# Hybrid parts that begin with products of the unnormed x

## The reference, cut to what matters

```python
h = rms_norm_2(x, mix_norm[l])              # x * rsqrt(mean(x*x) + eps) * w
z = h @ w_in                                # 1024 x 3592
hq, hf, hi, hg, fq, fk, fv, ff = split(z)   # 4 x 512 | 3 x 512 | 8
logf_h = logaddexp(log(lb), log1p(-lb) + log_sigmoid(hf)); k_h = (1 - lb) * sigmoid(-hf)
q_h = silu(hq); o_h = hgrn2_chunk_scan(q_h, k_h, hi, logf_h)
o_h = rms_norm_2(o_h, out_norm_w) * silu(hg)
logf_f = log_sigmoid(ff + fox_bf)           # forget gates of 8 heads
o_f = forgetting_attention(fq, fk, fv, logf_f)
x = x + concat(o_h, o_f) @ w_out
```

## Time and profile before

| | us |
|---|---|
| median of 3 runs (2647.03 to 2649.49) | 2648.58 |
| the profiled execution | 2646.76 |
| span of its trace | 2645.0 |
| PE busy / weight loads busy | 2586.8 / 2520.4 |
| DVE busy / ACT busy / POOL busy | 1669.6 / 1357.4 / 147.3 |
| mean granted TensorE clock, share of full | 0.996 |

### The profile page before, as it was taken

The page is one execution under the profiler, slowest core; times in us unless marked ns, Lnnn a source line. Parts: engine busy times, 40 slices in busy tenths (PEclk is TensorE's granted clock), DMA queues, the critical chain, the costliest instruction groups (busy, mean ns, idle before and its releaser), DMA issues.

```text
span 2645.0 us, 48803 instructions
## 1 busy us (share of the span) xinstructions
PE 2586.8 (98%) x21554; PEld 2520.4 (95%) x21554; DVE 1669.6 (63%) x1988; ACT 1357.4 (51%) x1687; POOL 147.3 (6%) x227
## 2 busy tenths in 40 slices
PE   8999999999999999999999999999999999999998
PEld 8989999899998999999999999989999999999998
DVE  5667556575576755676646656766656657764764
ACT  5745545554456544664545445555445436554543
POOL 4400000000000000430000000000000000000000
PEclk9999999999999999999999999999999999999999
DMA  7515565456544564543666665444766755344763
GB/s 217 168 33 161 193 236 162 145 175 226 182 160 144 183 226 158 162 132 112 197 241 177 192 224 179 129 159 133 199 195 185 198 192 160 112 143 130 195 195 128
DMA packets 429971, 451.97 MB, mean 171 GB/s; under 512 B 13346, under 2 KB 395024, under 8 KB 427584
## 3 DMA queue, kind: packets, MB, share of 16 engines
q1 hardware_dynamic: 417952, 416.12, 50.4%
q0 software_dynamic: 7312, 32.35, 3.5%
q10 hardware_dynamic: 4496, 0.39, 0.1%
HBM read 441.21 MB, written 7.60 MB: 170 GB/s over the span
## 4 chain that ended last, share of the span: by engine, by line
PE 86%; DVE 6%; ACT 5%; issue 1%; DMA 1%; POOL 1%; ACTq 0%; SPq 0%; DVEq 0%; POOLq 0%
PE ps L610 85%; ACT wH L1514 2%; DVE wL L2164 2%; ACT hidden_parts L1574 1%; DMA ring<-in_gdn_w_in 0%; POOL arena L512 0%; DVE arena L2737 0%; ACT L1541 0%; PE ps L1041 0%; DVE hT L2420 0%; PE ps L1259 0%; DMA arena<-tiles_out 0%; DVE sq L2247 0%; DVE arena L2428 0%; ACT sq L1783 0%
## 5 line engine op out<-in xcount | busy, mean ns | idle before, releaser
L2164 DVE TENSOR_TENSOR wL<-ring,wH 128x2048 fp32r<-128x2048 f32 x392 | 898.2, 2292 | 740.9 <-ACT wH L1514 740.5
L1514 ACT ACTIVATE wH<-ring 128x2048 fp32r<-128x2048 f32 x392 | 753.3, 1922 | 990.7 <-PE ps L610 988.7
L610 PE MATMUL ps<-hidden_parts,wH 128*128 128x256 f32 x6656 | 990.3, 277 | 4.4 <-ACT hidden_parts L1574 3.0
L610 PEld LDWEIGHTS ps<-hidden_parts,wH 128*128 128x128 f32 x6656 | 900.3, 188 | 6.4 <-issue 3.8
L610 PE MATMUL ps<-hidden_parts,wL 128*128 128x256 f32 x3328 | 693.3, 276 | 1.4 <-DVE wL L2164 1.3
L610 PEld LDWEIGHTS ps<-hidden_parts,wL 128*128 128x128 f32 x3328 | 521.9, 188 | 1.8 <-DVE wL L2164 1.8
L610 PE MATMUL ps<-hH,wH 128*128 128x256 f32 x2624 | 366.8, 281 | 6.8 <-DVE hH L2181 3.4
L610 PE MATMUL ps<-hH,wL 128*128 128x256 f32 x2624 | 358.3, 278 | 1.5 <-DVE wL L2164 1.5
L610 PE MATMUL ps<-hL,wH 128*128 128x256 f32 x2624 | 346.1, 278 | 0.0
L610 PEld LDWEIGHTS ps<-hH,wH 128*128 128x128 f32 x2624 | 328.5, 189 | 15.5 <-issue 13.2
L610 PEld LDWEIGHTS ps<-hH,wL 128*128 128x128 f32 x2624 | 326.1, 188 | 2.1 <-DVE wL L2164 2.0
(11 more groups left out here) (323 smaller groups left out, 1969.3 us busy)
## 6 DMA issues: line engine op xcount, KB each, us to landing
ring<-in_mlp_w SPq DMA_DIRECT2D x128, 1024.0 KB, 5.3
ring<-in_ffn_w_gate SPq DMA_DIRECT2D x88, 512.0 KB, 4.0
ring<-in_ffn_w_up SPq DMA_DIRECT2D x88, 512.0 KB, 5.3
ring<-in_ffn_w_down SPq DMA_DIRECT2D x44, 1024.0 KB, 5.1
ring<-in_gdn_w_in SPq DMA_DIRECT2D x32, 1024.0 KB, 5.9
ring<-in_w_in SPq DMA_DIRECT2D x28, 1024.0 KB, 5.4
hidden_parts<-mem_parts POOLq DMA_DIRECT2D x14, 1024.0 KB, 6.8
ring<-in_mlstm_w_in SPq DMA_DIRECT2D x12, 1024.0 KB, 5.3
```

What stands on the lines that cost most here:

```text
L610: return pe.matmul(o, l, r, start=start, stop=stop, **k)
L1514: f(wH[:, n % PARTS, :], ring[:, n % RING, :], ACT.Copy).then_inc(sem("high_split"), 1)
L2164: tt(wL[:, n % PARTS, :], ring[:, n % RING, :], wH[:, n % PARTS, :].bitcast(F32), ALU.subtract)\
```

## The change

- ACT (`late_start`) copies x times the norm's weights into `start_x[0]` (fp32r) instead of squaring first, empties the filler, makes the high part of slab 1, then squares xT, loads the table for ln and exp, and makes rs.
- DVE makes `start_x[1]`, the low part of slab 1, and the sum of squares over the chunks (`late_low`), then splits the 64 x 128 forget gate weights in two (`fox_w`).
- PE runs the whole filler first, then slab 0 alone, then slab 1; the two matmuls that end the sum of squares stand behind slab 1's products with the low part of x. The forget gates are 24 fp32r matmuls.
- Slabs 0 to 3 use `start_x`. DVE multiplies their sums by rs on the way from PSUM into qk (`scaled_out`), which ACT did without rs; ACT applies Silu to slabs 2 and 3 in SBUF.
- hT is still made (DVE, `normed`), and hH and hL from it (`normed_high` on ACT, `normed_low` on DVE) for slab 4 and later. PE waits for all of it ahead of slab 4.
- `start_x` lies where v_tok and gate are, so GpSimd's clearing of these waits for PE's end of slab 3.

```diff
+        start_x = (hidH[:, 24:32, :], hidH[:, 16:24, :])
+        fox_w = [flat_parts[:, at:at + DC * 8].rearrange("p (c n) -> p c n", c=DC) for at in (15424, 15488)]
 # GpSimd, hybrid
                     W.chain(pool.memset(qk[64:128, 12:16, :], 0.0))
+                    pool.wait_ge(sem("products_done"), group("w_in_2", i, HYBRID_ORDER[3]))
                     W.chain(pool.memset(gate[0:64, 4:8, :], 0.0))
 # TensorE, first_products
                 for k in range(DC):
                     both_halves(1, high_w[1], xL, k)
+                if behind_high:
+                    behind_high()
                 pe.wait_ge(sem("low_split"), n[1] + 1)
 # TensorE, hybrid
-                norm_sum(behind=6, filler=filled_before[("hybrid", l)], at=(0, 0, 0, 0, 10))
-                first_products("w_in_2", l, HYBRID_ORDER[0:2], DC, columns)
+                fill(filled_before[("hybrid", l)], 0, 2 * MEM_PIECES)
+                first_products("w_in_2", l, HYBRID_ORDER[0:2], DC, columns, src=start_x,
+                               together=False, behind_high=summed_norm)
...
-                        for k in range(DC):
-                            last = mm(ps[0:8, 0, 0:T], gw[:, 3 + l, k, 0:8], hT[:, k, :], k == 0, k == DC - 1)
+                        pe.wait_ge(sem("gate_split"), W.next("gate_split"))
+                        last = three(ps[0:8, 0, 0:T], [lambda k: fox_w[0][:, k, :], lambda k: fox_w[1][:, k, :]],
+                                     [lambda k: start_x[0][:, k, :], lambda k: start_x[1][:, k, :]], DC)
                     if n >= 4:
-                        pe.wait_ge(sem("evac"), W.next("evac"))
-                    (to_tokens if s in (4, 5) else to_channels)("w_in_2", l, s, bank_of(n))
+                        pe.wait_ge(sem("scaled_out"), W.next("scaled_out"))
+                    if n == 4:
+                        pe.wait_ge(sem("normH_ready"), W.next("normH_ready", 4))
+                        pe.wait_ge(sem("normL_ready"), W.next("normL_ready", 4))
+                    (to_tokens if s in (4, 5) else to_channels)("w_in_2", l, s, bank_of(n),
+                                                                src=start_x if n < 4 else (hH, hL))
 # ScalarE
+            def late_start(name, layer, j, gain, k0, filler):
+                for c in range(4):
+                    act.wait_ge(sem("x_ready"), W.next("x_ready"))
+                    for k in (2 * c, 2 * c + 1):
+                        ins = f(start_x[0][:, k, :], xT[:, k, :], ACT.Copy, scale=column(gain, k0 + k))
+                    ins.then_inc(sem("hH_ready"), 1)
+                empty_filler(filler)
+                split(slab_no[(name, layer, j)] + PARTS)
+                for c in range(4):
+                    f(sq[:, 2 * c:2 * c + 2, :], xT[:, 2 * c:2 * c + 2, :], ACT.Square).then_inc(sem("xsq_ready"), 1)
+                ln_exp()
+                act.wait_ge(sem("ss_ready"), W.next("ss_ready"))
+                rsqrt(ps[:, 2, 0:T], rs[:, :], D, "rs_ready")
 # ScalarE, hybrid
-                x_norm("w_in_2", l, HYBRID_ORDER[0], filler=filled_before[("hybrid", l)])
-                channels("w_in_2", l, 1, 4, chunks(qk, 4))
+                late_start("w_in_2", l, HYBRID_ORDER[0], "mix_norm_2", l * DC, filled_before[("hybrid", l)])
+                for n in range(2):
+                    ready("w_in_2", l, HYBRID_ORDER[n])
+                act.wait_ge(sem("scaled_out"), W.next("scaled_out", 2))
                 W.chain(f(glog, qk[:, 4:8, :], ACT.Abs))
                 W.chain(f(glog, glog, ACT.Exp, scale=-1.0))
                 f(glog, glog, ACT.Ln, bias=1.0).then_inc(sem("glog_ready"), 1)
+                normed_high()
 # VectorE, hybrid
-                x_norm("mix_norm_2", l * DC, "w_in_2", l, HYBRID_ORDER[0])
+                late_low("mix_norm_2", l * DC, start_x, "w_in_2", l, HYBRID_ORDER[0])
+                dve.wait_ge(sem("gates_in"), GATE_LOADS)
+                W.chain(dve.tensor_copy(fox_w[0], gw[:, 3 + l, :, 0:8]))
+                tt(fox_w[1], gw[:, 3 + l, :, 0:8], fox_w[0].bitcast(F32), ALU.subtract).then_inc(sem("gate_split"), 1)
...
                 dve.memset(pair[:, 0:4, :], 0.0)
...
+                refill("w_in_2", l, HYBRID_ORDER[0])
+                dve.wait_ge(sem("rs_ready"), W.next("rs_ready"))
+                scaled_out(0)
+                scaled_out(1)
+                normed("mix_norm_2", l * DC)
                 refill("w_in_2", l, 3)
                 dve.wait_ge(sem("gates_done"), W.next("gates_done"))
-                ts(r(1), ps[0:8, 0, 0:T], gbias[:, 2 + l:3 + l], None, ALU.add).then_inc(sem("fz_ready"), 1)
+                W.chain(tt(r(1), ps[0:8, 0, 0:T], rs[0:8, :], ALU.mult))
+                ts(r(1), r(1), gbias[:, 2 + l:3 + l], None, ALU.add).then_inc(sem("fz_ready"), 1)
+                normed_low()
                 dve.wait_ge(sem("glog_ready"), W.next("glog_ready"))
...
                 negative_cum(r(5)).then_inc(sem("rows_ready"), 1)
+                scaled_out(2)
                 refill("w_in_2", l, 0)
+                scaled_out(3)
```

More of the change, by code:

```diff
@@ L640, in bank_of, with first_products @@
                 return 4 + j % 4
-            def first_products(name, layer, js, c, at, src=(hH, hL), together=True):
+            def first_products(name, layer, js, c, at, src=(hH, hL), together=True, behind_high=None):
                 n = [slab_no[(name, layer, j)] for j in js]
@@ L1345, in hybrid @@
                     if n == 2:
-                        pe.wait_ge(sem("gates_in"), GATE_LOADS)
-                        for k in range(DC):
-                            last = mm(ps[0:8, 0, 0:T], gw[:, 3 + l, k, 0:8], hT[:, k, :], k == 0, k == DC - 1)
+                        pe.wait_ge(sem("gate_split"), W.next("gate_split"))
+                        last = three(ps[0:8, 0, 0:T], [lambda k: fox_w[0][:, k, :], lambda k: fox_w[1][:, k, :]],
+                                     [lambda k: start_x[0][:, k, :], lambda k: start_x[1][:, k, :]], DC)
                         last.then_inc(sem("gates_done"), 1)
                     if n >= 4:
-                        pe.wait_ge(sem("evac"), W.next("evac"))
-                    (to_tokens if s in (4, 5) else to_channels)("w_in_2", l, s, bank_of(n))
+                        pe.wait_ge(sem("scaled_out"), W.next("scaled_out"))
[4 more added lines that the diff above has]
+                                                                src=start_x if n < 4 else (hH, hL))
                 to_channels("w_in_2", l, 8, 1)
@@ L1564, in x_norm, with normed_high @@
                 empty_filler(filler)
+            def late_start(name, layer, j, gain, k0, filler):
[11 more added lines that the diff above has]
+                rsqrt(ps[:, 2, 0:T], rs[:, :], D, "rs_ready")
+            def normed_high():
+                for c in range(4):
+                    act.wait_ge(sem("h_ready"), W.next("h_ready", 2))
+                    f(hH[:, 2 * c:2 * c + 2, :], hT[:, 2 * c:2 * c + 2, :], ACT.Copy).then_inc(sem("normH_ready"), 1)
             def late_norm(name, layer, gain, k0, x_parts, between, filler=None):
@@ L1998, in hybrid @@
             def hybrid(l):
-                x_norm("w_in_2", l, HYBRID_ORDER[0], filler=filled_before[("hybrid", l)])
-                channels("w_in_2", l, 1, 4, chunks(qk, 4))
-                act.wait_ge(sem("evac"), W.next("evac", 2))
+                late_start("w_in_2", l, HYBRID_ORDER[0], "mix_norm_2", l * DC, filled_before[("hybrid", l)])
+                for n in range(2):
+                    ready("w_in_2", l, HYBRID_ORDER[n])
+                act.wait_ge(sem("scaled_out"), W.next("scaled_out", 2))
                 W.chain(f(glog, qk[:, 4:8, :], ACT.Abs))
@@ L2018, in hybrid @@
                 f(qk[:, 4:8, :], qk[:, 4:8, :], ACT.Sigmoid, scale=-1.0).then_inc(sem("hk_ready"), 1)
-                channels("w_in_2", l, 0, 6, chunks(qk, 0), func=ACT.Silu)
+                for s in range(2):
+                    ready("w_in_2", l, s)
+                    act.wait_ge(sem("scaled_out"), W.next("scaled_out"))
+                    v = qk[:, 2 * s:2 * s + 2, :]
+                    f(v, v, ACT.Silu)
                 channels("w_in_2", l, 3, 4, chunks(gate, 0), func=ACT.Silu)
@@ L2058, in hybrid @@
                         attention_slab(SLAB_ENDS[n - 1])
-                W.next("evac", 12)
                 square_pair(0, two(ps[:, 0, :]), "o_ready")
@@ L2197, in x_norm, with late_low @@
                     split(slab_no[(name, layer, j)] + PARTS)
-            def late_low(gain, k0, x_parts, name, layer):
+            def late_low(gain, k0, x_parts, name, layer, j=0):
                 for c in range(4):
@@ L2205, in late_low, with normed, normed_low @@
                     ins.then_inc(sem("hL_ready"), 1)
-                split(slab_no[(name, layer, 0)] + PARTS)
+                split(slab_no[(name, layer, j)] + PARTS)
                 sum_squares("xsq_ready", "xsq_summed")
+            def normed(gain, k0):
+                for c in range(DC):
```

(20 more changed lines are left out.)

## The result

| | before | changed |
|---|---|---|
| median of 15 runs | 2646.04 us | 2652.08 us |
| the profiled execution, its span | 2646.76, 2645.0 | 2651.15, 2649.4 |
| DVE busy / ACT busy | 1669.6 / 1357.4 | 1688.1 / 1361.9 |
| mean granted clock of TensorE | 0.996 | 0.993 |

The ratio is 1.0025, 95% interval 1.0019 to 1.0032: slower by some 6.6 us (5.0 to 8.5). Every ratio in this document is to runs of the kernel before that were taken beside it.

A forecast was written before the change was run, and what follows sets the result against it. PE was taken as the bound behind slab 5, with DVE exactly as late in front of it. Second part +2.5, first +0.3 and clock +1.0 made +3.8 us on 2648.58: 2652.4, range 2645.5 to 2657.

The forecast's parts named there:

- The start, the sum of squares, the gates: Layer 1: first product 1.06 us behind ACT, sum of squares ready 10.6 behind, gates 2.7 us on PE.
- the walk: Step-by-step timing of the first hybrid part: products start at the filler's end, 1613.6; PE asks for slab 4's low part at 1641.2.
- the list of signs: Expected trace evidence: first product 1.1 us behind ACT in both parts, waits in slabs 4 and 5, DVE without idle.
- DVE's run: DVE's work from low part 2 to the end of low part 4, without a gap: 20.4 us in layer 1.
- GpSimd's three later clearings: Clearings that fall beside DVE's run from about 2215 in layer 1; claimed to cost nothing.
- The waits: PE waits for DVE's low parts: in slab 4, 5.2 us (layer 1) and 3.1 (layer 0), then again in slab 5.
- The second wait: PE's wait for the low part of slab 5: 2.8 us in layer 1, 1.1 in layer 0.
- The clock: PE's pauses lower its granted clock; a later wait covers part of the loss; 1.0 us in all.
- The sum: Second hybrid part +2.5, first +0.3, clock +1.0: +3.8 us for the kernel.
- no change: A difference within 0.2%, 5.3 us, about what a measurement can tell from none; chance 0.62.
- The first rival: The early start stays because DVE's run is shorter, low part 4 ready when PE asks: -11 us, to 2637.6; chance 0.12.
- each earlier microsecond of PE is only a longer wait: At slab 4 in layer 1, the start's gain is gone, since PE must wait about 5.2 us for DVE's low part.

The follow-up runs named there:

- e1_pads_late: The changed kernel, with GpSimd's three clearings waiting for slab 8 instead of slab 3; 2649.66 us, ratio 1.0013 to the kernel before.
- e2_pe_busy: The changed kernel, with unread float32 matmuls on PE ahead of slab 4 (5 in layer 0, 11 in layer 1); ratio 1.0022 to the kernel before.
- e5_low_first: e1_pads_late with all work kept, low parts of slabs 4 to 7 made earlier on DVE, their high parts earlier on ACT; 2640.16 us, ratio 0.9975.
- e7_eighth_slab: e5_low_first with slab 8's high part on ACT and low part on DVE also made earlier; 2638.17 us, ratio 0.9965 to the kernel before.
- e4_gates_alone: The kernel before with only the forget gates changed, to 24 fp32r matmuls from hH and hL; 2641.89 us in one execution, no interval.
- e3_narrow_norm: e1_pads_late with DVE making hT and its low part for only 8 of 256 tokens; ratio 0.9987 to the kernel before.
- e6_low_first_pads: e5_low_first, but GpSimd's clearings wait for slab 3 as in the changed kernel; ratio 0.9971 to the kernel before.

## Why the prediction was right, and where it was off

**The number.** 2652.4 was forecast, with 2645.5 to 2657 as the range, and 2652.08 was measured. That the medians agree so closely is luck: the runs of the kernel before that stand beside it had a median of 2646.04, not 2648.58, and the forecast difference was +3.8 against some +6.6.

**The start, the sum of squares, the gates: right.** In layer 1, first product 1.06 behind ACT (I had 1.06), the two sum matmuls at 2200.60, 10.9 behind ACT's first copy (10.6), gates 2.8 for 2.7, slab 4 asking for its low part 29.0 behind for 29.1. In layer 0 the first product came 6.05 behind, at the filler's end, as the walk had it; the list of signs, with 1.1 in both parts, was wrong there. In that walk the terms up to PE's asking in layer 0 add up to 1641.05, not 1641.2.

**DVE's run: right but for one term.** I summed 20.4 us from low part 2 to the end of low part 4; to DVE's next record it was 2226.0 - 2203.8 = 22.2 in the changed kernel and 20.1 with the clearings out of the way. The term that failed is the one I set at nothing: "GpSimd's three later clearings fall beside DVE's run now ... I take nothing." It cost 2.1 in layer 1 and 0.6 in layer 0, 2.7 in all. I had compared a low pass beside a clearing with one without and taken that for all of DVE's operations. It holds for tensor_tensor, scalar_tensor_tensor and the scan, which kept their lengths; tensor_scalar was never beside a clearing in the kernel before. The Trainium skill names two cases of contention in "GPSIMD Engine Reference", section 1 (Specifications): a DVE instruction in a two-port perf mode, or with two SBUF inputs. I weighed the second alone. The runs do not show it, and they do show a slowing of tensor_scalar (0.35 to 1.0 us for one of 128x256); "VectorE: DVE Perf Modes" (Mode 2x_2P) says that float32 tensor_scalar is one of the operations that use both read ports, which agrees. That the ports are the cause is not shown here; that the clearings are is shown by e1_pads_late.

**The waits: the first right in kind, the second covered.** I had 5.2 and 3.1 in slab 4; it was 5.24 and 3.01 without the clearings, 7.33 and 3.61 with them. The second wait, 2.8 and 1.1, was there as 1.14 and 0.74 in e1_pads_late. In the changed kernel the slow clock took its place: no record of layer 0 shows it, and in layer 1 PE's low products of slab 5 start within 0.05 of the end of low part 5, 1.17 behind the group before them instead of 0.91.

**The clock: the mechanism right, the size about right.** I had 1.0 in all. Taken by itself it cost nothing to speak of in layer 1 (0.1 by e2_pe_busy) and 1.3 in layer 0. But it cost that only because the clearings had made layer 0's wait longer: without them, in e1_pads_late, layer 0 kept the full clock and layer 1's loss was covered.

**The sum: one term missing, and two errors that cancel.** 2.5 + 0.3 + 1.0 = 3.8 was forecast; with 2.7 for the clearings it is 6.5, and 6.3 was measured in the parts. That this fits is in part luck. Without the clearings (e1_pads_late) the parts are 0.1 and 1.9 longer than before, 2.0 in all where I had 3.8: the waits cost 0.8 less than I had, and the clock cost nothing. The clearings then cost 4.3 of the parts and not 2.7, since in layer 0 they also brought the fall of the clock. The difference, 6.6 us, is on the side forecast and most likely past the 5.3 us (0.2%) that I called no change and had held likeliest (0.62), though its interval begins at 5.0; without the clearings it would have been within.

**The first rival: right to reject, for too narrow a reason.** It needed DVE's run to be 5 us shorter, and it isn't. But the low parts do not need the whole run: e5_low_first and e7_eighth_slab get most of the 11 us by order alone. And my sentence that each earlier microsecond of PE is only a longer wait holds for the changed order, not for the kernel before, where e4_gates_alone gained 1.4 in layer 1 before DVE's idle time was used up. I had read the 0.84 of idle time in the earlier trace rows as almost no room, and had not asked what DVE waited for in it.

## What to carry to other kernels

When PE is given an earlier start, sum what the feeding engine has between two things that PE asks for, and put what PE asks for first: the same work in another order, the clearings moved too, turned +6.6 us into about -9. A wait that shows as 0.2 us may hide an engine fed by PE itself; look one step further back in the chain before calling it the bound. When an edit moves work of GpSimd, look for each kind of DVE operation that it will lie beside, not for one of them.

## What the runs showed of the hardware

- Clearings of 128x1024 and 64x1024 on GpSimd (0.95 to 0.98 us each) lengthened DVE's tensor_scalar records beside them from 0.35 to some 1.0 us (128x256, three records of the changed kernel) and from 0.28 to 0.88 (8x256), and left tensor_tensor, scalar_tensor_tensor and scan records alone. A copy was lengthened too: in e4_gates_alone the copy of 128x64 took 0.63 us beside a clearing in layer 0 and 0.19 with none beside it in layer 1.
- After PE waits of 7.33, 3.61 and 5.24 us the granted clock was at its lower level (1.2 GHz); after one of 3.01 it stayed at 2.4 GHz, after ones of 2.92 (e2_pe_busy) and 2.78 (e3_narrow_norm) it had fallen. So the length of the wait alone does not say it.
- PE's groups of 8 matmuls run in one of two paces at the full clock, 0.907 or 0.94 us, and change from one to the other at a single record. The program does not settle it: slabs 4 to 7 have the same matmuls in e5_low_first, e6_low_first_pads and e7_eighth_slab, and ran at 0.94 throughout in the first and at 0.907 in layer 0 of the other two. Nor does a wait: behind one of 0.74 us in layer 0 came 0.907 in e1_pads_late and 0.94 in e2_pe_busy. What did set it to 0.907 is one matmul of 64 columns: in the kernel before, groups 0.94 apart stand ahead of such a one at 551.36 us and groups 0.907 apart behind it. The cause was not found.

```profile
1650.66 1.20 PE L613 MATMUL ps<-hH,wL 128*128 128x256 f32 x8 [0.74 <-DVE wL L2198]
1651.70 1.07 PE L613 MATMUL ps<-hH,wH 128*128 128x256 f32 x8
...
1653.96 1.21 PE L613 MATMUL ps<-hH,wL 128*128 128x256 f32 x8 [0.74 <-DVE wL L2200]
1655.01 1.10 PE L613 MATMUL ps<-hH,wH 128*128 128x256 f32 x8
```
